# Branch merge by halves with split products, 512-column output projections fed in pieces, and a latent mask applied by VectorE

## What is computed

```python
# 1 merge of the hybrid mixer (y_pool, hm: 1024 x 512)
y_a = y_pool @ w_br_a ; y_b = hm @ w_br_b
merged = sigmoid(h @ w_ga) * y_a + sigmoid(h @ w_gb) * y_b
# 2 projection and residual, then an RMS norm
x = x + merged @ w_out
# 3 after each of the two attentions of the second block
x = x + attended @ w_out
# 4 latent attention, 16 heads, causal, keys and queries of 96
s = q @ k.T ; s[key later than query] = -inf ; p = exp(s - max) ; o = p @ v / sum(p)
```

## Time and profile before

| | us |
|---|---|
| median of 3 runs (lowest to highest) | 2963.41 (2960.33 to 2964.24) |
| the profiled execution | 2962.59 |
| its span on the core | 2960.9 |
| merge, matmuls from / to | 380 / 671 |
| first projection, matmuls from / to | 683 / 789 |
| output projection of the first attention | 2178 / 2276 |
| latent attention, scores from / to | 2522 / 2854 |
| output projection of the latent attention | 2854 / 2952 |

### The profile page before, as it was taken

The page is one execution under the profiler, slowest core; times in us unless marked ns, Lnnn a source line. Parts: engine busy times, 40 slices in busy tenths (PEclk is TensorE's granted clock), DMA queues, the critical chain, the costliest instruction groups (busy, mean ns, idle before and its releaser), DMA issues. The chain is left out here.

```text
span 2960.9 us, 36884 instructions
## 1 busy us (share of the span) xinstructions
PE 2618.3 (88%) x12888; PEld 2080.1 (70%) x12888; DVE 1481.8 (50%) x2708; ACT 1179.9 (40%) x1693; POOL 447.5 (15%) x373
## 2 busy tenths in 40 slices
PE   4999789997849999999549999688898898899998
PEld 3887656667738888888437887377898786466578
DVE  3542711213459999999550340576533224555623
ACT  5222411101327777777351351232323235344531
POOL 0000000000003233332100360233220000022220
PEclk8999889998969999999769999898999999999999
DMA  3111021103339999999452590666630412000131
GB/s 97 36 43 29 1 72 43 43 15 121 114 126 392 377 380 377 375 387 384 186 161 89 150 288 28 169 156 158 153 117 1 137 25 40 5 16 18 39 107 58
DMA packets 263102, 408.14 MB, mean 138 GB/s; under 512 B 86107, under 2 KB 179931, under 8 KB 262844
## 3 DMA queue, kind: packets, MB, share of 16 engines
q1 hardware_dynamic: 230768, 334.45, 34.3%
q0 software_dynamic: 20784, 54.62, 5.9%
q10 hardware_dynamic: 11420, 17.32, 2.0%
HBM read 354.85 MB, written 66.46 MB: 142 GB/s over the span
## 5 line engine op out<-in xcount | busy, mean ns | idle before, releaser
L3250 ACT ACTIVATE lattn_pT<-ps 128x512 f32<-128x512 f32 (+1 forms) x160 | 91.9, 575 | 174.6 <-PE ps L3193 173.6
L157 DVE TENSOR_TENSOR moe_wg_low<-moe_wg_raw,moe_wg_high 128x1024 fp32r<-128x1024 f32 x128 | 148.3, 1220 | 20.5 <-ACT moe_wg_high L1359 20.4
L157 DVE TENSOR_TENSOR moe_wd_low<-moe_wd_raw,moe_wd_high 128x1024 fp32r<-128x1024 f32 x128 | 150.9, 1223 | 8.4 <-ACT moe_wd_high L1359 8.4
L3207 PE MATMUL ps<-lattn_pT,c_v 128*65 128x512 f32 (+3 forms) x384 | 150.5, 487 | 0.0
L157 DVE TENSOR_TENSOR moe_wu_low<-moe_wu_raw,moe_wu_high 128x1024 fp32r<-128x1024 f32 x128 | 148.3, 1221 | 0.9 <-ACT moe_wu_high L1359 0.6
L150 PE MATMUL ps<-ab_h,abp_w 128*128 128x512 f32 x336 | 134.9, 401 | 3.5 <-DVE abp_w L157 3.5
L151 PE MATMUL ps<-ab_h,abp_w 128*128 128x512 f32 x336 | 134.3, 400 | 0.0
L152 PE MATMUL ps<-ab_h,abp_w 128*128 128x512 f32 x336 | 134.1, 399 | 0.0
L1359 ACT ACTIVATE moe_wg_high<-moe_wg_raw 128x1024 fp32r<-128x1024 f32 x128 | 125.0, 1055 | 11.2 <-DMA moe_wg_raw<-in_w_e_gate_dram 11.2
L1359 ACT ACTIVATE moe_wd_high<-moe_wd_raw 128x1024 fp32r<-128x1024 f32 x128 | 128.1, 1053 | 0.0
L2416 PE MATMUL ps<-att_qx,att_kx 65*128 65x256 f32 (+1 forms) x512 | 114.5, 358 | 14.0 <-DVE att_sT L2611 14.0
(11 more groups left out here) (552 smaller groups left out, 7660.0 us busy)
## 6 DMA issues: line engine op xcount, KB each, us to landing
moe_wg_raw<-in_w_e_gate_dram SPq DMA_DIRECT2D x128, 512.0 KB, 8.3
moe_wu_raw<-in_w_e_up_dram SPq DMA_DIRECT2D x128, 512.0 KB, 8.2
moe_wd_raw<-in_w_e_down_dram SPq DMA_DIRECT2D x128, 512.0 KB, 9.0
qk_parts<-abp_high POOLq DMA_DIRECT2D x58, 256.0 KB, 12.4
qk_parts<-abp_full POOLq DMA_DIRECT2D x58, 256.0 KB, 12.2
abp_raw<-in_ab_w_in_dram SPq DMA_DIRECT2D x22, 512.0 KB, 5.2
proj_w_raw<-in_w_in_dram SPq DMA_DIRECT2D x20, 512.0 KB, 4.0
merge_raw<-in_w_in_dram SPq DMA_DIRECT2D x16, 512.0 KB, 6.2
```

Of the source, the lines that this page charges most:

```text
L157: return dve.tensor_tensor(low, x, high.bitcast(F32), ALU.subtract)
L3207: mm = pe.matmul(ps[0:C_V + 1, acc + half, q0 + skip - half * HALF:HALF], v, pT[:, g % SUMS, off + skip:off + n], start=(b == 0), stop=(j ...
L3250: act.activation(pT[:, g % SUMS, 0:total], ps[:, 4 + g % 2, 0:total], ACT.Exp, scale=C_SCALE).then_inc(e_done, 1)
```

## The change

- Merge: the halves become the outer loop (16 rounds r, one half and one tile j each), the gate weights are so loaded and split twice over. The branch products become split products: 12 matmuls of 512 columns in the place of 4 plain ones. ACT and DVE split the branch weights of a round (one instruction each, 1024 elements a partition) and, before the first and the ninth round, the branch inputs (8 instructions of 512 each). Two raw buffers in the place of three.
- First projection: 2 chunks of 512 columns, fed in 4 pieces of two slices k each; one set of split weights, replaced piece by piece as TensorE finishes with them in the last token tile.
- Output projections: the same chunks and pieces. In chunk 0 tiles 0 to 3 take slices 0 to 6, then tiles 4 to 7, then all take slice 7. Chunk 1 runs over the first four slices for all tiles, then over the last four.
- Latent attention: the mask matmuls go. DVE adds the mask to the 128 x 128 diagonal block in PSUM between scores and Exp; two of the products with 256 columns a head become 128 wide.

```diff
 # mixer_merge, TensorE
-                for j in range(KT):
+                for r in range(ROUNDS):
+                    base = 4 * (r % 2)
                     for which in range(2):
...
-                            for k in range(4):
-                                mm = pe.matmul(ps[:, base + 2 + which, :], wb[:, j % 2, which, k, :], src[:, k, cols], start=(k == 0), stop=(k == 3))
+                        if which == 0:
+                            pe.wait_ge(wb_split, r + 1)
+                        for k in range(4):
+                            if r % KT == 0:
+                                pe.wait_ge(src_split, 8 * (r // KT) + 4 * which + k + 1)
+                            mm = multiply_split(pe, ps[:, base + 2 + which, :], (wb_high[:, r % 2, which, k, :], wb_low[:, r % 2, which, k, :]),
+                                                (src_high[:, which, k, :], src_low[which][:, k, cols_of(r)]), k == 0, k == 3)
 # mixer_merge, ScalarE
+                for r in range(ROUNDS):
+                    if r == KT:
+                        act.wait_ge(done, 4 * KT)
+                        high_source(r, 0)
+                        high_source(r, 1)
...
+                    if r + 1 < ROUNDS:
+                        high_branch(r + 1)
 # project_norm, ScalarE
+                def high_piece(p):
+                    if PIECES <= p < 2 * PIECES - 1:
+                        act.wait_ge(w_used, p - PIECES + 1)
+                    elif p == 2 * PIECES - 1:
+                        act.wait_ge(done, NT)
+                    k = 2 * (p % PIECES)
+                    act.wait_ge(loaded[p % 2], 16 * (p // 2 + 1))
+                    act.activation(w[:, 0, k:k + 2, :], raw[:, p % 2, :, :], ACT.Copy).then_inc(w_high, 1)
+                high_rows(0)
+                for p in range(PIECES):
+                    high_piece(p)
+                for t in range(1, NT):
+                    high_rows(t)
 # project_norm, VectorE
+                            if n + 1 < CHUNKS and s == NT - 1:
+                                for p in range(PIECES, 2 * PIECES - 1):
+                                    low_piece(p)
                             dve.wait_ge(done, u + 1)
...
+                            if n + 1 < CHUNKS and s == NT - 1:
+                                low_piece(2 * PIECES - 1)
 # multiply_out
+    for half in range(2):
+        if half:
+            pe.wait_ge(banks_free, 2 * KT)
+        for k in range(KT - 1):
...
+            for t in range(4 * half, 4 * half + 4):
+                mm = product(t, k)
+            if half and k == OUT_KH - 1:
+                mm.then_inc(O["w_used"], 1)
+    pe.wait_ge(O["m_split"], KT)
+    for t in range(NT):
+        product(t, KT - 1).then_inc(O["done"], 1)
+    for kh in range(2):
+        for t in range(NT):
+            if kh == 0:
+                pe.wait_ge(O["added"], t + 1)
...
 # add_out
-        if t == 0 and n + 2 < OUT_CHUNKS:
-            for p in (2 * n + 4, 2 * n + 5):
-                if n:
-                    low_out_weights(dve, O, p)
+        if n == 0:
+            for p in (4, 5):
+                low_out_weights(dve, O, p)
...
+        if n == 0:
+            for p in (6, 7):
+                low_out_weights(dve, O, p)
 # latent_attention
-        plan = [... [(2, 0, 2 * P), (3, 0, 2 * P)], ... [(6, 1, 2 * P), (7, 1, 2 * P)]]
+        plan = [... [(2, 0, 2 * P), (3, 0, P)], ... [(6, 1, 2 * P), (7, 1, P)]]
-                            pe.matmul(ps[:, 4 + g % 2, off:off + 2 * P], identity[:, :], mask[:, seen:seen + 2 * P], start=True, stop=False, skip_group_check=True)
 # latent_attention, ScalarE
+                        if diagonal[g % NGH]:
+                            act.wait_ge(masked, masks_until(g))
+                        else:
+                            act.wait_ge(s_made, g + 1)
 # latent_attention, VectorE, ahead of the items of group g
+                        if diagonal[g % NGH]:
+                            dve.wait_ge(s_made, g + 1)
+                        for off in diagonal[g % NGH]:
+                            block_s = ps[:, 4 + g % 2, off:off + P]
+                            dve.tensor_tensor(block_s, block_s, mask[:, :], ALU.add).then_inc(masked, 1)
```

More of the change, by code:

```diff
@@ L856, in _ @@
                     if which == 0:
[L857 to L860, removed]
+                        if r >= 2:
+                            sp.wait_ge(done, 4 * (r - 1))
+                        for b, branch in enumerate((w_br_a, w_br_b)):
+                            sp.dma_start(wb_raw[:, r % 2, b, :, :], tiled_rows(branch[:, j * P:(j + 1) * P])).then_inc(wb_loaded[r % 2], 16)
@@ new lines, in _ @@
+                        s = n % 3
+                        if which == 0 and r >= 2:
+                            pe.wait_ge(out_sem, r - 1)
+                        for k in range(KT):
+                            mm = multiply_split(pe, ps[:, base + which, :], (w[:, s, 0, k, :], w[:, s, 1, k, :]), (h[:, 0, k, cols_of(r)], h[:, 1, k, cols_of(r)]),
+                                                k == 0, k == KT - 1)
+                        mm.then_inc(done, 1)
+                        if which == 0:
+                            pe.wait_ge(wb_split, r + 1)
@@ new lines, in _ @@
+                for r in range(ROUNDS):
+                    if r == KT:
+                        low_source(r, 0)
+                        low_source(r, 1)
+                    for which in range(2):
+                        n = 2 * r + which
+                        if n + 3 < 2 * ROUNDS:
+                            low_weights(dve, W, n + 3)
+                        dve.wait_ge(sig, n + 1)
+                        dve.wait_ge(done, 2 * n + 2)
+                        link(dve.tensor_tensor(part[:, which, :], ps[:, 4 * (r % 2) + 2 + which, :], sg[:, which, :], ALU.mult))
+                    dve.tensor_tensor(mT[:, r % KT, cols_of(r)], part[:, 0, :], part[:, 1, :], ALU.add).then_inc(out_sem, 1)
+                    dve.wait_ge(out_sem, r + 1)
+                    if r + 1 < ROUNDS:
+                        low_branch(r + 1)
@@ L990, in _, with low_rows @@
             def _(dve):
[L991 to L999 removed]
+                def low_rows(t):
                     cols = slice(t * P, (t + 1) * P)
@@ L3091, in pieces, with masks_until @@
             return out, off
+        diagonal = [[off for b, half, q0, n, off in pieces(units)[0] if q0 == b * P] for units in plan]
+        def masks_until(g):
+            return NT * (g // NGH) + sum(len(d) for d in diagonal[:g % NGH + 1])
         with nc.Block() as block:
```

314 lines of the change are left out of this document (149 added, 165 removed).

## The result

| | before | after |
|---|---|---|
| median, us (lowest to highest) | 2963.12 (2960.33 to 2964.24) | 2911.24 (2908.94 to 2912.10) |
| the profiled execution | 2962.59 | 2911.78 |
| its span | 2960.9 | 2910.1 |

The ratio is 0.9825 (interval 0.9808 to 0.9842): 51.9 us faster. I had forecast 2907 (2896 to 2928), 56.7 us faster.

What follows compares the result with a forecast made beforehand. TensorE's summed instructions were taken to set the time. Savings of 20.0 + 8.5 + 7.8 + 7.8 + 12.6 = 56.7 us from 2962.6 gave 2905.9, with the median 0.8 above: 2907 us; range 2899 to 2915, wider 2896 to 2928.

Steps and rivals of the forecast that it cites:

- its two reasons: Lower end of the wider range, 2896 us: no mask waits in the latent attention, and narrow products at half price.
- the cover: Merge: TensorE's work hides the added copies and splits; taken as 0, bounds 0 to +6 us at each of two places.
- The waits for pieces: First projection, in the middle: TensorE waits 1.7 us at piece 7 of 8 and 0.7 at piece 8.
- 383 x 0.233 = 89.2: Output projections: 383 starts of 512-column matmuls at 0.233 us each; -8.1 us, with +0.3 for the add -7.8 a site.
- The stall: Output projection of the first attention: a 3.97 us stall, laid to VectorE standing at two splits for chunk 3, goes.
- a rival by which only stalls go: Matmuls of 512 columns cost twice those of 256: +8 us, 2915 us in all; chance 0.04.
- 0.1 to 0.2 for each late low part: Latent attention: exposed wait per late low part; with 0.1 to 0.2 a head, 3.6 us in all.
- The sign that I had named: Latent attention: TensorE's waits on Exp, above all after line 3320 and after low parts, would prove the forecast wrong.
- VectorE is no bound: Rival: VectorE bounds the latent attention, masks, line 3320 and low parts all waited for, 74 us; 2977 us, chance 0.03.
- the masks are not exposed one by one: Rival: in the latent attention the masks alone are exposed, 36 us of waits instead of 3.6; 2939 us, chance 0.11.
- the pieces come in time: Rival: four reloads in the first projection come too slowly, 23 us instead of 5; 2925 us, chance 0.07.
- the merge's inputs are hidden: Rival: the splits of the merge's inputs are in the open at both places; 2919 us, chance 0.05.

Runs made afterwards that it cites:

- e1: Kernel before with only the merge by halves and its split branch products: 2950.01 us, ratio 0.9942.
- e7: Kernel after with the merge's branch products plain again, the low parts of their operands left out of the product: 2930.00 us, ratio 0.9888.
- e5: Kernel after with low parts of output weights and finished rows, weight loads and ScalarE's high parts of the weights at other places: 2904.79 us, ratio 0.9798.
- e4: Kernel before with only the latent mask on VectorE and the two narrower products, old output projection kept: 2959.36 us, ratio 0.9979.
- e11: Kernel after, unchanged, run and profiled once more: 2914.46 us, ratio 0.9819.
- e8: Kernel after with every latent mask added twice by VectorE, the second add waiting for the first: 2927.06 us, ratio 0.9871.
- e6: Kernel after with two paddings alone, 96 bytes a partition in the merge and 32 in the first projection: 2909.49 us, ratio 0.9820.
- e10: Kernel after with moved low parts, three raw buffers in the first projection, paddings in merge, ab projections and experts' last product: 2902.45 us, ratio 0.9791.

## Why the prediction was right, and where it was off

The forecast of the whole was 4.8 us too large, and that is two errors in opposite directions. The changed stages gained 58.8 us in the profile (22.5, 8.0, 10.7, 6.9 and 10.7) where I had summed 56.7; the span fell by 50.8, so the stretches that nothing was changed in gave 8.0 back. That the sum came within 5 us is luck in part. (The lower end of the wider range, 2896, does not follow from its two reasons: 3.6 and 5.0 off 2907 give 2898.)

- **Merge**, forecast 20.0: 20.3 (e1). Every step held: the block, no wait at either place where the inputs are split, the cover. e7 shows that the rest of the rewriting costs nothing.
- **First projection**, forecast 8.5: 10.2 in the change (30.5 for the first two columns, less the 20.3 of e1), 11.7 alone. The waits for pieces were there, 1.62 and 1.34 where I had 1.7 and 0.7. The first tile took 9.7 us against 9.3 by my dates. The mis-sized term is the rate: seven tiles ran 38.1 us, where 5.59 each make 39.1.
- **Output projections**, forecast 7.8 each: 10.7 and 10.6. The step that failed is "383 x 0.233 = 89.2". I took the rate of 512 columns from the merge, the nearest row with that shape; here they start 0.227 apart, so 383 take 86.9. The stall went as I said, with no other in its place. A pair of 256 columns takes 0.240 and one of 512 takes 0.227, so that each of the 384 instructions saved is worth 13 ns and not 7. The estimate from the Trainium skill (TensorE: Matmul & The Clock Gate, "Back-to-back issue gap"), which I set aside, had the whole sum 5 us smaller, and the measured rates lie on the other side. I had also named a rival by which only stalls go, with 512 columns at twice 256: it is out by 5.1 us a site.
- **Latent mask**, forecast 12.6: 6.9. Of the 16.2 us taken from TensorE I had counted 3.6 as lost, and 9.3 are (the parts below come to 9.5). The settled heads are right: 0.87 us gained in each against the 0.9 forecast, which loses 0.14 a head of the 1.01 taken out, 1.4 in ten of them. The step that failed is "0.1 to 0.2 for each late low part". I had found half of the mechanism, a mask behind a low part with Exp waiting, and priced it by the slack of 1.8 us that I had read in a settled head. The sign that I had named came: waits on Exp of 4.5 us over the last heads, where 1.5 were. The other half I had not seen: low part and mask also delay the row maxima, and that is most of the loss from head 12 to 14. By the steps of heads, 0.4 are lost from head 12 to 13, 2.4 from 13 to 14 (20.84 became 22.27) and 3.5 behind the last head's keys (52.0 became 52.9, for 2.6 heads of work), where no matmuls of a next head stand between two scores. Of these 6.3 e5 gets back 3.4 by other places for the low parts (and for the loads and ScalarE's high parts of the weights; 0.7, 2.35 and 1.4, less 1.0 given back from head 14 to 15); e4 shows that it comes with the masks. 1.8 more are lost in the first two heads (1.2 in the profile of e4), which no run took apart.
- **The unchanged stretches**, forecast as the same: 8.0 us longer in this profile, 5.6 of it in the score phase. e11 has this phase 3.4 us longer still, so it varies by some us from one execution of a kernel to the next; but whether the change adds to it stays open. The 5.6 are idle time of TensorE (34.2 us for 28.1). Its waits on VectorE (`att_sT`) are 17.8, 15.9 and 15.5 us where the phase takes 256.0, 259.4 and 259.1, so they alone don't set its length; the granted clock has a share too.

The rivals: VectorE is no bound (39.3 of 40 us are TensorE's), the masks are not exposed one by one (e8 shows how near that is, though at the row maxima and not at Exp), the pieces come in time but for 4.2 us, and the merge's inputs are hidden.

## What to carry to other kernels

Price a matmul by the distance of its starts at the site that will run it, or at one with the same operands, since one shape has more than one rate in one kernel. When an engine with idle time takes over work on a critical path, go through its queue at the stretch that is least like the settled one: work of another kind that stands ahead of it there (here the low parts of the next stage) can cost more than the work itself (3.5 us in the last head, where a mask takes 0.3), and the wait may fall on another consumer of the same queue than the one that you watch. Moving that work by a few places won 4.4 us here and cost 1.0. And judge a few microseconds by the stages that were changed: the rest of one and the same program varied by more.

## What the runs showed of the hardware

- fp32r matmuls of 128 rows by 512 columns start 226.7 ns apart at some sites and 233.3 at others (544 and 560 cycles of 2.4 GHz, worked out): in the output projections and the latent gates the one, in the merge's gates and the ab projections the other, with one site between, at 228.9. An unedited site keeps its rate from one profile to the next. Paddings moved three sites, by -1.2, -0.9 and +3.4 ns (e6, e10); the rest is open.
- fp32r matmuls of 128 columns start 111 ns apart (the ab products, `ps<-abp_w,ab_h`) and those of 256 columns 120 (the old projections), so halving 256 columns brings 9 ns.
- A plain float32 product of the same size takes 0.86 us, 3.7 times one of them; three of them are still cheaper.
- A mask add, with one operand in PSUM and one in SBUF, takes 0.30 us also inside an operation of POOL (at 2601.56, where POOL works from 2600.20 to 2602.55); a low part of rows, with both inputs in SBUF, that begins inside an operation of POOL ends 1.08 us after it (three cases; 3.34, 2.14 and 2.82 us instead of 1.23), and a tensor_tensor of 8 columns 0.02 to 0.03 us after it (thirteen cases in the kernel before, up to 2.16 us instead of 0.17).
